# Block one's query, hyena, Fourier and gate projections as three products of rounded parts, with four load places

## The reference, cut to what matters

```
mx = silu(c) @ w_mod + b_mod; sh1, sc1, g1, sh2, sc2, g2 = split(mx)     # modulation
hx = rms_norm(x, norm1_g) * (1 + sc1) + sh1
p  = hx @ w_in                    # 1024 x 4864: q 512, k 128, v 128, hyena 768, fourier 256, gates 3072
att = attention(q, [k, k_ctx], [v, v_ctx])    # k_ctx, v_ctx from the context tokens
hy  = hyena(p[hyena])             # short convolution, two long convolutions by spectrum, with a filter from a small MLP
fn  = fft2(p[fourier]).real
m   = sigmoid(ga) * (att @ wb1) + sigmoid(gh) * (hy @ wb2) + sigmoid(gf) * (fn @ wb3)
x   = x + g1 * (m @ w_out)
x   = x + g2 * expert_choice_moe(modulate(rms_norm(x), sh2, sc2))     # 16 experts, 24 MB of weights each
```

## Time and profile before

| | us |
|---|---|
| median of three runs | 2506.03 |
| profiled execution: its own time | 2498.66 |
| profiled execution: span of the trace | 2497.3 |
| PE busy | 2083.5 (83%) |
| DVE busy | 928.9 (37%) |
| ACT busy | 605.7 (24%) |
| mean granted PE clock, of full speed | 0.897 |

### The profile page before, as it was taken

The page is one execution under the profiler, slowest core; times in us unless marked ns, Lnnn a source line. Parts: engine busy times, 40 slices in busy tenths (PEclk is TensorE's granted clock), DMA queues, the critical chain, the costliest instruction groups (busy, mean ns, idle before and its releaser), DMA issues.

```text
span 2497.3 us, 28539 instructions
## 1 busy us (share of the span) xinstructions
PE 2083.5 (83%) x12064; PEld 1376.1 (55%) x12064; DVE 928.9 (37%) x1193; ACT 605.7 (24%) x748; POOL 62.3 (2%) x147
## 2 busy tenths in 40 slices
PE   5889998866666666766668999999999999999998
PEld 3556685211111111111114899777998899777997
DVE  2531323000000000000000665875657665875656
ACT  2121011000000000000000444464445444454444
POOL 0000000000000000000000000100000000100000
PEclk9898998887777777677779999999999999999999
DMA  8224445999999999999999455315555355315552
GB/s 311 95 81 185 153 174 205 398 421 421 421 421 421 421 421 421 421 421 421 421 422 419 176 194 180 124 67 194 195 185 193 137 194 179 133 60 191 195 186 93
DMA packets 93255, 647.39 MB, mean 259 GB/s; under 512 B 11495, under 2 KB 12424, under 8 KB 16328
## 3 DMA queue, kind: packets, MB, share of 16 engines
q1 hardware_dynamic: 89856, 639.93, 65.2%
q10 hardware_dynamic: 3272, 5.64, 0.7%
HBM read 644.48 MB, written 1.05 MB: 258 GB/s over the span
## 4 chain that ended last, share of the span: by engine, by line
PE 53%; DMA 33%; DVE 8%; ACT 2%; issue 1%; POOL 1%; ACTq 1%; SPq 1%; DVEq 0%; POOLq 0%
PE PS L829 11%; PE PS L830 11%; PE PS L831 11%; DMA ring<-in_md 8%; DMA ring<-in_mu 7%; PE PS L400 4%; DMA mix<-in_mu 2%; DMA XT<-in_mu 2%; DMA XT<-in_md 2%; PE PS L792 2%; DVE low L1636 2%; PE PS L758 1%; DMA HRI<-in_mu 1%; DMA tables<-in_mu 1%; DMA QT<-in_mu 1%
## 5 line engine op out<-in xcount | busy, mean ns | idle before, releaser
L1636 DVE TENSOR_TENSOR low<-ring,WH 128x2048 fp32r<-128x2048 f32 (+1 forms) x164 | 374.4, 2283 | 188.2 <-ACT WH L1993 185.4
L829 PE MATMUL PS<-XH,WH 128*128 128x256 f32 x1408 | 398.1, 283 | 5.0 <-DVE XL L1654 5.0
L830 PE MATMUL PS<-XL,WH 128*128 128x256 f32 x1408 | 398.0, 283 | 0.0
L831 PE MATMUL PS<-XH,low 128*128 128x256 f32 x1408 | 397.3, 282 | 0.0
L1993 ACT ACTIVATE WH<-ring 128x2048 fp32r<-128x2048 f32 (+1 forms) x164 | 313.2, 1910 | 25.3 <-DMA ring<-in_fg 19.6
L829 PEld LDWEIGHTS PS<-XH,WH 128*128 128x128 f32 x1408 | 267.4, 190 | 9.4 <-issue 8.1
L830 PEld LDWEIGHTS PS<-XL,WH 128*128 128x128 f32 x1408 | 266.2, 189 | 1.4
L831 PEld LDWEIGHTS PS<-XH,low 128*128 128x128 f32 x1408 | 266.9, 190 | 0.0
L1618 DVE TENSOR_TENSOR SS<-SS,PS 128x512 f32<-128x512 f32 x16 | 11.0, 688 | 551.8 <-PE PS L758 551.8
L758 PE MATMUL PS<-ring,big 128*32 128x512 f32 x928 | 151.2, 754 | 63.9 <-DMA ring<-in_mu 42.6
L792 PE MATMUL PS<-ring,PT 128*32 128x512 f32 x480 | 101.7, 874 | 60.6 <-DMA ring<-in_md 52.7
(11 more groups left out here) (385 smaller groups left out, 2587.2 us busy)
## 6 DMA issues: line engine op xcount, KB each, us to landing
ring<-in_mu SPq DMA_DIRECT2D x62, 1024.0 KB, 26.5
ring<-in_md SPq DMA_DIRECT2D x60, 1024.0 KB, 27.0
ring<-in_mg SPq DMA_DIRECT2D x54, 1024.0 KB, 26.7
ring<-in_fg SPq DMA_DIRECT2D x44, 1024.0 KB, 4.9
ring<-in_fu SPq DMA_DIRECT2D x44, 1024.0 KB, 4.9
ring<-in_fd SPq DMA_DIRECT2D x44, 1024.0 KB, 4.8
ring<-in_wmod SPq DMA_DIRECT2D x24, 1024.0 KB, 6.9
XT<-in_mg SPq DMA_DIRECT2D x21, 1024.0 KB, 27.0
```

What stands on the lines that cost most here:

```text
L829: t.matmul(o, l[0], r[0], start=start, stop=False, skip_group_check=True)
L830: t.matmul(o, l[0], r[1], start=False, stop=False, skip_group_check=True)
L831: return t.matmul(o, l[1], r[0], start=False, stop=stop, skip_group_check=True)
L1636: own(v.tensor_tensor(low[:, w.slot.index, 0:size], w.flat, WH[:, w.slot.index, 0:size].bitcast(f32), ALU.subtract).then_inc(*c.wl.up()), ...
```

## The change

Places 4 and 5 of the ring are taken out of the cycle of block one's early loads, which turn in places 0 to 3. For each of the 18 tiles of `wq`, `why`, `wfn` and `wgt` (`early`), ACT copies the tile, rounded, into `low[:, 4 + n % 2]` (n its number), and DVE subtracts that from the tile and writes the rest over it. `XT` is likewise parted into `XTH` (over `masks` and `pT`, whose loads now wait for gate 12) and `XTL` (over `XT`, after the last read of it by keys/values). `mm3` then makes each product. The parts are called at fixed points of the two orders: two ahead of XTH and XTL, one after the rotary tables, one at the start of each hyena tile and of the Fourier tile, and one within each of gates 0 to 10, for the next. The rotary tables move behind XT2, and PE makes the context transposes 0 and 1 before its first step of q. The gate rows get a place of their own and come two mods later in the queue. Places 4 and 5 come back for `wbr`.

```diff
@@ memory @@
-        masks = sb("masks", [128, 2, 2, 256])
-        pT = sb("pT", [128, 2, 2, 256])
+        with ExitStack() as raw:
+            masks = sb("masks", [128, 2, 2, 256], f32, raw)
+            pT = sb("pT", [128, 2, 2, 256], f32, raw)
+        XTH = sb("XTH", [128, 8, 256], f32r)
-            XT = sa("XT", [128, 8, 256])
+            with ExitStack() as raw:
+                XT = sb("XT", [128, 8, 256], f32, raw)
+            XTL = sb("XTL", [128, 8, 256], f32r, first)
+            bias = sa("bias", [128, 512])
@@ the queue @@
+        def load_early(name, i, used, value):
+            load(name, i, used, value)
+            W[name, i].tile = len(early)
+            early.append(W[name, i])
+
+        slots = cycle[0:4]
         for n in range(4):
             load_mod(n)
         load("wkv", 0, c.kv, 4)
         for i in range(2):
-            load("wq", i, c.q, 3 + i)
+            load_early("wq", i, c.q, 3 + i)
         for n in range(3):
-            load("why", n, c.hy, n + 1)
-        load("wfn", 0, c.fn, 1)
+            load_early("why", n, c.hy, n + 1)
+        load_early("wfn", 0, c.fn, 1)
         for n in range(12):
-            load("wgt", n, c.gt, n + 1)
+            load_early("wgt", n, c.gt, n + 1)
+            if n + 3 in GATE:
+                load("bmodg", GATE[n + 3] * 2 + (n + 3) % 2, c.mod, n + 4, bias_slot)
             if n < 8:
                 load_mod(n + 4)
+        for i in range(2):
+            cycle[4 + i].first = early[16 + i].used
+        slots = slots[0:2] + cycle[4:5] + slots[2:3] + cycle[5:6] + slots[3:4]
@@ tensor_program @@
+            def early_parts(name, i):
+                w = W[name, i]
+                P.wait_ge(c.wl, w.tile + 1)
+                return [low[:, at, :].rearrange("p (a b) -> p a b", a=w.src.shape[1]) for at in (4 + w.tile % 2, w.slot.index)]
             def q_work():
+                P.wait_ge(c.xtv, 3)
...
-                        i = t.matmul(PS[:, m, :], XT[:, k, m * 128:m * 128 + 128], w.ap[:, k % 4, :], start=k == 0, stop=k == 7)
+                        w = early_parts("wq", k // 4)
+                        i = mm3(PS[:, m, :], [x[:, k, m * 128:m * 128 + 128] for x in (XTH, XTL)],
+                                [x[:, k % 4, :] for x in w], k == 0, k == 7)
             def feature_rows(name, n, b):
...
-                        x = t.matmul(PS[:, b, i * 256:i * 256 + 256], w.ap[:, k, i * 128:i * 128 + 128], XT[:, k, :],
-                                     start=k == 0, stop=k == 7)
+                        x = mm3(PS[:, b, i * 256:i * 256 + 256], [y[:, k, i * 128:i * 128 + 128] for y in w],
+                                [XTH[:, k, :], XTL[:, k, :]], k == 0, k == 7)
...
-                step()
+                if j == 1:
+                    step(2)
@@ vector_program @@
+            def part():
+                nonlocal parted
+                w = early[parted]
+                V.wait_ge(c.wh, parted + 1)
+                own(v.tensor_tensor(low[:, w.slot.index, :], w.flat, low[:, 4 + parted % 2, :].bitcast(f32),
+                                    ALU.subtract).then_inc(*c.wl.up()), c.wl)
+                parted += 1
             def hyena(n):
+                part()
                 for _ in range(4):
                     yield 1
                 V.wait_ge(c.hy, n + 1)
             def gate(n):
-                for _ in range(4):
+                for i in range(4):
+                    if n < 11 and i == (2 if n < 8 else 0):
+                        part()
                     yield 1
...
-            V.wait_ge(*l_filt)
-            rope_tables()
+            for _ in range(2):
+                part()
+            V.wait_ge(c.xta, 3)
+            V.wait_ge(c.kv, 2)
+            own(v.tensor_tensor(XTL[:, :, :], XT[:, :, :], XTH[:, :, :].bitcast(f32), ALU.subtract).then_inc(*c.xtv.up()), c.xtv)
             for j in (0, 2):
                 V.wait_ge(c.xtp, j + 9)
...
+            V.wait_ge(*l_filt)
+            rope_tables()
+            part()
@@ scalar_program @@
+            def part():
+                nonlocal parted
+                w = early[parted]
+                A.wait_ge(*w.landed)
+                if parted > 1:
+                    A.wait_ge(*early[parted - 2].used)
+                own(copy(low[:, 4 + parted % 2, :], w.flat).then_inc(*c.wh.up()), c.wh)
+                parted += 1
...
+            for _ in range(2):
+                part()
+            A.wait_ge(c.xtv, 2)
+            own(copy(XTH[:, :, :], XT[:, :, :]).then_inc(*c.xta.up()), c.xta)
@@ sync_program @@
                 if n == experts_from:
+                    S.wait_ge(c.gt, 12)
```

More of the change, by code:

```diff
@@ L23 @@
 rr gm act pool out rg xsa l_c2T l_x l_id l_sel2 l_ctx l_gain l_filt l_hyc l_hyl l_masks l_row ring0 ring1 ring2
-ring3 ring4 ring5 wide0 wide1 wide2 wide3 wide4 wide5 wide6
+ring3 ring4 ring5 bias wide0 wide1 wide2 wide3 wide4 wide5 wide6
 """
@@ L253, in load_mod @@
                 load("wmod", 2 * n + kh, c.modmm, 2 * n + kh + 1)
-            if n in GATE:
-                load("bmodg", GATE[n] * 2 + n % 2, c.mod, n + 1)
+        early = []
+        bias_slot = [Slot(bias, c.bias)]
+        def load_early(name, i, used, value):
[3 more added lines that the diff above has]
+        slots = cycle[0:4]
         for n in range(4):
@@ L295, in load_split @@
             load(name, i, c.wu, len(split) + 1)
-            W[name, i].tile = len(split)
+            W[name, i].tile = len(early) + len(split)
             split.append(W[name, i])
@@ L419, in fourier_in @@
             def fourier_in():
-                w = W["wfn", 0]
                 take(7)
-                P.wait_ge(*w.landed)
+                w = early_parts("wfn", 0)
                 for m in range(2):
                     for k in range(8):
-                        x = t.matmul(PS[:, 7, m * 256:m * 256 + 256], XT[:, k, m * 128:m * 128 + 128], w.ap[:, k, :],
-                                     start=k == 0, stop=k == 7)
+                        x = mm3(PS[:, 7, m * 256:m * 256 + 256], [y[:, k, m * 128:m * 128 + 128] for y in (XTH, XTL)],
+                                [y[:, k, :] for y in w], k == 0, k == 7)
                         if k == 3 or (k == 7 and m == 0):
@@ L523, in keys_values @@
                     for k in range(8):
-                        P.wait_ge(c.xta if k // 2 % 2 else c.xtv, 2 * half + k // 4 + 1)
+                        P.wait_ge(c.xta if k // 2 % 2 else c.xtv, 3 * half + k // 4 + 1)
                         x = t.matmul(PS[:, 4 + half, m * 256:m * 256 + 256], src[:, k, m * 128:m * 128 + 128],
@@ L539, in tensor_program @@
                 x.then_inc(*c.xtp.up())
-                held[b] = [(c.xta, j // 2 + 3) if j % 2 else (c.xtv, j // 2 + 3)]
-                step()
+                held[b] = [(c.xta, j // 2 + 4) if j % 2 else (c.xtv, j // 2 + 4)]
+                if j == 1:
+                    step(2)
             drain()
@@ L826, in parts @@
                         for x in (WH, low)]
[L828 to L831, removed]
             def rows(m, j, b, src, count, value):
@@ L1634, in split_to @@
                     size = w.flat.shape[-1]
-                    V.wait_ge(c.wh, ready + 1)
+                    V.wait_ge(c.wh, len(early) + ready + 1)
                     own(v.tensor_tensor(low[:, w.slot.index, 0:size], w.flat, WH[:, w.slot.index, 0:size].bitcast(f32),
@@ L1640, in tile @@
             def tile(name, i):
-                return W[name, i].tile
+                return W[name, i].tile - len(early)
             def gains(m, j, b, g):
@@ L2008, in mod @@
                 yield 1
+            parted = 0
+            def part():
[6 more added lines that the diff above has]
+                parted += 1
             def hyena(n):
+                part()
                 for _ in range(4):
@@ L2130, in scalar_program @@
             const("selb", selb[:, :], l_hyc)
-            A.wait_ge(c.ra, 1)
-            own(a.activation(sn[:, :, :], ang, ACT.Sin))
-            own(a.activation(cs[:, :, :], ang, ACT.Sin, scale=0.5).then_inc(*c.rsin.up()), c.rsin)
+            for _ in range(2):
+                part()
+            A.wait_ge(c.xtv, 2)
+            own(copy(XTH[:, :, :], XT[:, :, :]).then_inc(*c.xta.up()), c.xta)
             for j in (1, 3):
@@ L2138, in scalar_program @@
                            modT[:, 2 * j + 1, 1:2]).then_inc(*c.xta.up()), c.xta)
+            A.wait_ge(c.ra, 1)
+            own(a.activation(sn[:, :, :], ang, ACT.Sin))
+            own(a.activation(cs[:, :, :], ang, ACT.Sin, scale=0.5).then_inc(*c.rsin.up()), c.rsin)
+            part()
             filt, side, filtering = filters(), beside2(), True
```

12 lines of the change are left out of this document (7 added, 5 removed).

## The result

The changed kernel takes 2510.69 us (median of 17 runs, 2505.98 to 2519.87), the kernel before beside it 2503.17 (17 runs, 2495.61 to 2510.41): a ratio of 1.0036 between the means, 95% interval 1.0024 to 1.0048. It is slower: by 7.5 us between the medians, 9.0 between the means. The prediction had called 7.5 us the border of what one measurement tells from no change; with 17 runs of each the interval excludes no change. Its profiled execution took 2519.87 us (span 2518.5), the slowest of the 17.

What follows compares the result with a forecast made beforehand. Expert weights bound the expert stage, and block one's shifts before about 370 us move everything after. Terms -0.7 +14.4 -7.2 +6.5 -0.9 -4.7 sum to +7.4 on 2506.03, so 2513 us; range 2495 to 2524.

Steps and rivals of the forecast that it cites:

- To 77 us: Start of block one through keys/values and q: -0.7 us, with q's products -2.4 and a PE wait of 1.7.
- 77 to 149 us: Hyena and Fourier stretch: +14.4 us, +11.5 from DVE delays behind late parts and +2.9 from PE's half clock.
- The signs named: Changed trace, 77 to 149 us: DVE gap 6 to 9 us, sine 86.5, PE idle 8, reciprocal near 142.7, L482 near 149.
- Attention: 149 to 262 us: PE bounds it, the parts are hidden, 26 pieces gain 0.3 us each less small waits, -7.2.
- rival B: Attention loses its cover: DVE's parts delay operations PE waits for, the -7.2 is lost, 2521 us; chance 0.20.
- sign of being wrong: Sine within 3 us of the VV copy, attention stretch not shorter, or anything behind the first expert differing.
- The start at half clock: PE after its 5 us wait before L482: 6 us at half rate, costing +2.9 us.
- Long convolution: 262 to 315 us: gt7's late load and part delay the spectrum product and PE, +6.5; then three pieces -0.9.
- last four gates: 64 products fall from 27.63 to 22.9 us, -4.7; gt10's and gt11's parts are ready before a gate ends.
- Rival A: The parts hide in block one, gt7's too, so only the gains stay: -14.7, 2491 us; chance 0.20.

Runs made afterwards that it cites:

- the kernel with all three edits: Changed kernel with wkv loaded into HRI's memory, the hyena and Fourier tiles' parts called earlier, and gate 7's part behind the spectrum product: 2484.32 us, ratio to before 0.9938.

## Why the prediction was right, step by step

The time (2510.69 for 2513), the sign and the size of the shift (+8.7 at the first expert load in the profiled execution, 9.6 between the means of all traces, +7.4 forecast) are right. That the medians differ by 7.5 us, as forecast to 0.1, is luck: the means of the runs differ by 9.0, and the stages, -0.4 +10.1 -2.1 +2.0, miss the terms by up to 2.2 us both ways. The terms:

- **To 77 us**, -0.7: the VV copy moved from 77.42 to 77.09, by 0.4 between the means. Right.
- **77 to 149 us**, +14.4, of which +11.5 on DVE. The first stage grew by 10.1 us (65.6 for 55.5, means). The signs named came as written: gap of 5.27 us (6 to 9 forecast, the one miss: why1 landed in 4.7 us, not 5.6) and sine at 86.15 (86.5), PE idle 7.65 (8), reciprocal 142.75 (142.7), L482 at 149.07 (149) after a wait of 5.18 (5). But the price was laid out over single waits as if each stood by itself. The runs show one cause in two conditions: the part's place in DVE's and ACT's order, and the late load, give back 10 to 11 us together and 2 and 3.5 alone.
- **Attention**, -7.2: hidden as forecast. PE waits there 2.7, 1.6, 1.0, 1.0 us for the same operations as before (2.6, 1.6, 1.0, 1.0), so rival B's mechanism did not come. What failed is the size in time. From the reciprocal on the sum has +2.9 and -7.2, together -4.3; the means differ by 2.1 us (132.2 for 134.3), and single executions (133.2 after, 132.5 before) not even in sign, which the prediction had named as a sign of being wrong. The start at half clock came and was no longer than allowed: L510 took 3.78 us for 1.98, and by 153.24 instructions started 0.12 us apart again. What the sum lacks is the later falls, by which the stretch has a clock of 0.87 to 0.88 for 0.92 and 0.95.
- **Long convolution**, +6.5 - 0.9, and **last four gates**, -4.7, together +0.9; measured +2.0 (104.0 for 102.0). Landing 7.60 us, the upper end of the earlier trace rows; PT done at 290.3, 5.6 us late on its place; the transform at 6.78 us, not 5.41, for a wait of 6.37. Removing the wait gave 7.7 to 8.1, so this term was sized 1 to 1.5 us too low (its parts, +4.8 +1.9 -0.3, make 6.4). The gates took 22.6 (22.9). No wait came in them.
- **Rival A**, all parts hidden, 2491 us, 14.7 below: that is what the kernel with all three edits is. By the ratio of its runs it lies 15.5 us below (0.9938; the medians, 2484.32 and 2502.2 for the runs of the kernel before beside it, are 17.9 apart). Nothing in the change itself made A come.

That the waits around the parts, and not the work of rounding, decide was the right reading: the products give 16 us of time, and two places in the order and one load place cost over 20 (from 2510.69 to 2484.32). What stands behind the first expert load differs between the two profiled executions, another sign of being wrong, but by no more than executions of one kernel do.

## What to carry to other kernels

When a tile needs preparation by two engines before its product, cost not the preparation but what stands behind it in each engine's order: the same part (a landing, 1.9 us of ACT, 2.3 of DVE) added no wait in attention and cost 7.7 us ahead of one spectrum product. A load that waits for a place and a step that is placed early have to be mended together; trying one of them alone tells little. And a stage's gain on PE is worth only what the clock leaves: compare length times granted clock, and count the products in the stretch, before taking a difference of stages for an effect of the code.

## What the hardware showed that was not expected

One program's attention stage took 126.4 and 129.6 us in two executions, and one order of 692 instructions 126.6 and 133.2 in two kernels, with no wait in the trace to tell them apart but the granted clock (0.93 and 0.91, 0.92 and 0.87). And the rounded products lose less at half clock than the clock says: instructions of 256 columns start every 0.119 us at full clock, as in the earlier trace rows, and every 0.213 at half, 1.8 times. These are the starts after the wait of 7.65 us, where the granted clock of the stretch is 0.50:

```profile
91.26 0.41 PE L379 MATMUL PS<-XTH,low 128*128 128x256 f32 x1
91.47 0.41 PE L377 MATMUL PS<-XTH,low 128*128 128x256 f32 x1
91.69 0.41 PE L378 MATMUL PS<-XTL,low 128*128 128x256 f32 x1
```

```profile
89.70:95.50 5.80, 3.89 (x14) 2.84 (x14) 4.14 (x15) 0.12 (x1) 1.02 (x1) 0.50 0.15 27
```
